# Hybrid mixer backbone on one core: latent branch reordered, gate tiles ahead of the transposes, raw gate tiles, norm sums in buffers of their own

## The reference, cut to what matters

```
def qkv(dq, dkv, kr, rope_tabs, need_q):
    kv = (rms_norm(dkv, g_ckv) @ w_ukv).reshape(b, t, MLA_HEADS, MLA_NOPE + MLA_V)
    k  = rms_norm(concatenate([kv[..., :MLA_NOPE], k_r], -1), g_k)
    q  = rms_norm((rms_norm(dq, g_cq) @ w_uq).reshape(b, t, MLA_HEADS, 96), g_q)
    ...
g = sigmoid(gate_pre)         # 3 x 1024 gate channels, from the same input as q, k, v
y = (g_a * y_a + g_b * y_b + g_c * y_c) @ w_out
```

## Time and profile before

| | us |
|---|---|
| median of 3 runs (1823.93 to 1825.36) | 1824.24 |
| the profiled execution's own time | 1828.72 |
| its span in the profile | 1827.0 |
| latent branch, layer 0, first product to first score (439.60 to 593.06) | 153.5 |
| latent branch, layer 1 (1414.71 to 1526.76) | 112.1 |
| PE busy, share of the span | 1659.8, 91% |
| DVE, ACT, POOL busy | 969.2, 783.1, 668.7 |
| granted PE clock, mean (1 is 2.4 GHz) | 0.961 |

### The profile page before, as it was taken

One profiled execution on the slowest core, in us unless ns is written; L12 is line 12 of the kernel. 1 busy time (PEld: TensorE's weight loads), 2 busy tenths in 40 slices (PEclk: granted clock), 3 DMA queues, 4 the chain that ended last, 5 costly groups with the idle time before them and its releaser, 6 DMA issues.

```text
span 1827.0 us, 24655 instructions
## 1 busy us (share of the span) xinstructions
PE 1659.8 (91%) x9536; PEld 1394.2 (76%) x9536; DVE 969.2 (53%) x1751; ACT 783.1 (43%) x1484; POOL 668.7 (37%) x389
## 2 busy tenths in 40 slices
PE   7998989899878999899999998978899788889998
PEld 3876779767666667688888886968887676789998
DVE  5855816753235555359496964143135145556665
ACT  4334644343446442442323234247534465455443
POOL 0633344411234001345455543525541343034443
PEclk9999999999989999999999998989999898999999
DMA  8432434400122312224354743223420133245553
GB/s 334 188 138 89 177 113 170 150 24 24 61 87 89 125 66 100 77 92 164 136 200 169 276 165 112 87 81 108 130 93 24 65 121 126 79 139 185 185 184 116
DMA packets 69852, 230.63 MB, mean 126 GB/s; under 512 B 18281, under 2 KB 24809, under 8 KB 56425
## 3 DMA queue, kind: packets, MB, share of 16 engines
q1 hardware_dynamic: 60880, 213.67, 33.4%
q10 hardware_dynamic: 8856, 15.39, 2.4%
HBM read 216.45 MB, written 12.58 MB: 125 GB/s over the span
## 4 chain that ended last, share of the span: by engine, by line
PE 72%; DVE 10%; ACT 9%; issue 4%; POOL 3%; DMA 1%; SPq 0%; ACTq 0%; POOLq 0%; DVEq 0%
PE bank L1694 36%; PE bank L1732 8%; PE bank L1776 7%; PE bank L1714 4%; PE bank L2044 4%; PE bank L2023 3%; PE bank L1758 2%; PE bank L2030 2%; ACT wH L772 2%; POOL wL L659 1%; DVE acc L1165 1%; PE bank L1925 1%; DVE mjunk L1162 1%; ACT L798 1%; POOL wL L661 1%
## 5 line engine op out<-in xcount | busy, mean ns | idle before, releaser
L659 POOL TENSOR_TENSOR wL<-raw,wH 128x1280 fp32r<-128x1280 f32 (+4 forms) x146 | 307.8, 2108 | 612.3 <-ACT wH L772 612.3
L772 ACT ACTIVATE wH<-raw 128x768 fp32r<-128x768 f32 (+7 forms) x396 | 296.7, 806 | 486.0 <-PE bank L1694 351.1
L661 POOL TENSOR_TENSOR wL<-raw,wH 128x768 fp32r<-128x768 f32 (+3 forms) x198 | 322.8, 1630 | 368.5 <-ACT wH L772 368.4
L1694 PE MATMUL bank<-hH,wH 128*128 128x512 f32 (+1 forms) x720 | 246.8, 343 | 4.6 <-DVE oL L1557 2.9
L1694 PE MATMUL bank<-hL,wH 128*128 128x512 f32 (+1 forms) x720 | 245.2, 341 | 0.0
L1694 PE MATMUL bank<-hH,wL 128*128 128x512 f32 (+1 forms) x720 | 245.1, 340 | 0.0
L1694 PE MATMUL bank<-oH,wH 128*128 128x512 f32 (+1 forms) x576 | 197.0, 342 | 2.9 <-DVE oL L1557 2.9
L1694 PE MATMUL bank<-oL,wH 128*128 128x512 f32 (+1 forms) x576 | 195.7, 340 | 0.0
L1694 PE MATMUL bank<-oH,wL 128*128 128x512 f32 (+1 forms) x576 | 195.6, 340 | 0.0
L1165 DVE SCALAR_TENSOR_TENSOR acc<-acc,cb 128x1024 f32<-128x1024 f32 x88 | 170.9, 1955 | 2.5
L1732 PE MATMUL bank<-hH,wH 128*128 128x512 f32 (+1 forms) x384 | 142.4, 371 | 25.7 <-ACT gst L798 12.3
(11 more groups left out here) (217 smaller groups left out, 3258.3 us busy)
## 6 DMA issues: line engine op xcount, KB each, us to landing
raw<-in_p_ff SPq DMA_DIRECT2D x64, 1024.0 KB, 4.8
acc<-in_p_mod SPq DMA_DIRECT2D x44, 1024.0 KB, 5.7
raw<-in_p_ml SPq DMA_DIRECT2D x12, 1024.0 KB, 5.3
raw<-in_p_na SPq DMA_DIRECT2D x12, 1024.0 KB, 5.6
raw<-in_p_mgc SPq DMA_DIRECT2D x16, 512.0 KB, 3.6
raw<-in_p_mga SPq DMA_DIRECT2D x16, 512.0 KB, 3.5
raw<-in_p_mgb SPq DMA_DIRECT2D x16, 512.0 KB, 3.5
raw<-in_p_out SPq DMA_DIRECT2D x8, 1024.0 KB, 4.8
```

The source lines that it names most:

```text
L659: pool.tensor_tensor(l_[:, 0:cut], r_[:, 0:cut], h_[:, 0:cut].bitcast(F32), ALU.subtract)
L661: pool.tensor_tensor(l_[:, cut:k * w], r_[:, cut:k * w], h_[:, cut:k * w].bitcast(F32), ALU.subtract)\
L772: act.activation(flat(wH, n)[:, part], flat(raw, n)[:, part], ACT.Copy)\
L1694: ins = pe.matmul(dst, w_[:, kk, c:c + P], r_[:, kk, lo:TOK], start=kk == k0 and m == 0, stop=kk == k0 + kn - 1 and m == 2)
```

## The change

It concerns the latent branch of both layers, the gate tiles in it, and the start of `to`. What it does, part by part:

- **Norm.** ACT squares the first four chunks straight from PSUM, each into a buffer of its own (c_sq), and PE's sums stand between and behind the two halves of dk; the sum of the fifth stands between the two `cn` gate tiles. Chunks 0 to 2 (queries) and 3, 4 (keys) get their roots, scaling and split separately, and PE's first unit waits for the first three alone. The rotary key's squares are one instruction at the start, its sums one instruction, and its rotation stands ahead of DVE's work on the fifth chunk. Ln and Exp come after one table load.
- **Gate tiles.** `cn` has 2 in both layers (3 and 4 before); the units have 1 each in layer 0 (0, 2, 0, 1, 1, 1, 1, 1 before) and 2, 2, 1, 1, 1, 1 in layer 1 (1 each before). In a unit they stand ahead of the transposes. Tiles 16 to 23 are copied out raw (Copy in place of Tanh).
- **Units.** ACT does both squares, both roots, then the weight splits, the gates, and the two query copies of the unit before; DVE both sums, the two key copies of the unit before, then both scalings.
- **Merge.** ACT makes 8 Tanh over chunks of the branch-1 gate at the start of `to`, 4 ahead, into g_tanh; DVE waits for them.
- **Ring.** The order of blocks follows the new order, and with it the planner's slots. By L444 to L458 the changed releasers are, for layer 0 / 1: gate 16 by dk (both); gate 17 by gate 14 (both); uq0 by dq1 (both); gate 18 (layer 1), gate 19 (layer 0) by uq0; ukv (layer 1) by uq1 instead of gate 18; gate 20 (layer 1) by gate 18; wo0 by to2 instead of to1 (both); wo1 (layer 1) by wo0 instead of to3, since in layer 1 it now overlaps wo0's slots.

The diff, cut to its core:

```diff
-FILL = (dict(chain=3, loop=8, last=3, cn=3, units=(0, 2, 0, 1, 1, 1, 1, 1)),
-        dict(chain=3, loop=8, last=3, cn=4, units=(1, 1, 1, 1, 1, 1)))
+FILL = (dict(chain=3, loop=8, last=3, cn=2, units=(1, 1, 1, 1, 1, 1, 1, 1)),
+        dict(chain=3, loop=8, last=3, cn=2, units=(2, 2, 1, 1, 1, 1)))
+
+
+def untouched(l, T):
+
+    return T >= gate_range(l, 0).start
...
-        at = gate_range(l, 0).start
-        if l == 0:
-            load += [("uq", l, 0), g[at], g[at + 1], ("uq", l, 1), ("ukv", l, 0), *g[at + 2:]]
-            use += [("uq", l, 0), g[at], g[at + 1], ("uq", l, 1), *g[at + 2:at + 6], ("ukv", l, 0), *g[at + 6:]]
-        else:
-            load += [("uq", l, 0), g[at], ("uq", l, 1), g[at + 1], ("ukv", l, 0), *g[at + 2:]]
-            use += [("uq", l, 0), g[at], ("uq", l, 1), *g[at + 1:at + 5], ("ukv", l, 0), *g[at + 5:]]
+        stages = [("uq", l, k // 2 if l == 0 else k) for k in range(4 if l == 0 else 2)] + [("ukv", l, 0)] * 4
+        for k, key in enumerate(stages):
+            fill = [g[T] for T in gate_range(l, k)]
+            load += ([key] if stages.index(key) == k else []) + fill
+            use += ([key] if key not in stages[k + 1:] else []) + fill
...
+        c_sq = (s_sq, s_sq2, st[:, 0], st[:, 1], view(10752, 512))
...
+                    if untouched(l, T):
+                        ins = act.activation(gst[:, n % 2, t0:], bk, ACT.Copy)
+                    else:
+                        ins = act.activation(gst[:, n % 2, t0:], bk, ACT.Tanh, scale=0.5)
+                    ins.then_inc(S("gate_free").handle, 1)
...
-                        for j in range(3):
-                            ahead(N[("dq", l, j) if j < 2 else ("dk", l, 0)])
-                            if j < 2:
-                                for b in range(2):
-                                    c = 2 * j + b
-                                    lo = t0 if c < 3 else 0
-                                    act.activation(l_c[:, c, lo:], full(u0 + j, b)[:, lo:TOK], ACT.Copy)\
-                                        .then_inc(free(u0 + j, b), 1)
-
-                        for u, b in ((u0 + 1, 1), (u0 + 2, 1)):
-                            act.wait_ge(*S(f"bank_free{2 * (u % 2) + b}").at(u // 2 + 1))
-                        for c in range(5):
-                            lo = t0 if c < 3 else 0
-                            if c > 0:
-                                act.wait_ge(*S(tag + "csum").at(c))
-                            act.activation(s_sq[:, lo:], l_c[:, c, lo:], ACT.Square).then_inc(S(tag + "csq").up(1), 1)
-                        act.wait_ge(*S(tag + "csum").at(5))
-                        act.activation(st[:, 0, t0:], bank[4][:, t0:TOK], ACT.Ln, scale=1.0 / MLA_QR, bias=eps[:, 0:1])
-                        link(act.activation(st[:, 1, :], bank[5][:, :], ACT.Ln, scale=1.0 / MLA_KVR, bias=eps[:, 0:1]))
-                        act.activation(st[:, 0, t0:], st[:, 0, t0:], ACT.Exp, scale=-0.5)\
-                            .then_inc(S(tag + "cstd").up(1), 1)
-                        act.activation(st[:, 1, :], st[:, 1, :], ACT.Exp, scale=-0.5)\
-                            .then_inc(S(tag + "cstd").up(1), 1)
-                        act.preload_act_table_set("sqrt_and_others")
-                        for c in range(5):
+                        act.activation(l_t, small[:, :, 32:64], ACT.Square).then_inc(S(tag + "krs").up(1), 1)
+                        exp_and_ln()
+                        for j in range(2):
+                            for b in range(2):
+                                c = 2 * j + b
+                                lo = t0 if c < 3 else 0
+                                src = full(u0 + j, b)[:, lo:TOK]
+                                act.activation(c_sq[c][:, lo:], src, ACT.Square).then_inc(S(tag + "csq").up(1), 1)
+                                act.activation(l_c[:, c, lo:], src, ACT.Copy).then_inc(free(u0 + j, b), 1)
+                            ahead(N["dq", l, j])
+
+                        def deviations(q, lo, done):
+
+                            act.wait_ge(*S(tag + "csum").at(done))
+                            link(act.activation(st[:, q, lo:], bank[4 + q][:, lo:TOK], ACT.Ln,
+                                                scale=1.0 / (MLA_KVR if q else MLA_QR), bias=eps[:, 0:1]))
+                            act.activation(st[:, q, lo:], st[:, q, lo:], ACT.Exp, scale=-0.5)\
+                                .then_inc(S(tag + "cstd").up(1), 1)
+
+                        def latent_high(c):
+
                             lo = t0 if c < 3 else 0
                             act.wait_ge(*S(tag + "cn").at(c + 1))
                             act.activation(oH[:, C_AT[c], lo:], l_c[:, c, lo:], ACT.Copy).then_inc(S(tag + "cH").up(1), 1)
 
-                        for t in range(NTILE):
-                            act.activation(l_t[:, 0:ROPE], small[:, t, 32:64], ACT.Square).then_inc(S(tag + "krs").up(1), 1)
-                            act.wait_ge(*S(tag + "krsum").at(t + 1))
+                        deviations(0, t0, 3)
+                        act.wait_ge(*S(f"bank_free{2 * ((u0 + 2) % 2) + 1}").at((u0 + 2) // 2 + 1))
+                        act.activation(c_sq[4], l_c[:, 4, :], ACT.Square).then_inc(S(tag + "csq").up(1), 1)
+                        for c in range(3):
+                            latent_high(c)
+                        ahead(N["dk", l, 0])
+                        deviations(1, 0, 5)
+                        for c in (3, 4):
+                            latent_high(c)
                         gates_out(l, "cn")
+                        act.preload_act_table_set("sqrt_and_others")
...
+                    else:
+                        for k in range(len(nb) // 2):
+                            for m in (2 * k, 2 * k + 1):
+                                squared(m)
+                            for m in (2 * k, 2 * k + 1):
+                                deviation(m)
+                            u = u0 + 3 + k
+                            for key in (("uq", l, 0), ("uq", l, 1), ("ukv", l, 0)):
+                                if used[N[key]] == (f"bank_full{2 * (u % 2) + 1}", u // 2 + 1):
+                                    ahead(N[key])
+                            gates_out(l, k)
+                            if k:
+                                queries_out(2 * k - 2)
+                                queries_out(2 * k - 1)
+                        act.preload_act_table_set("exp_and_others")
...
+                def merge_tanh(c):
+
+                    act.wait_ge(*S(f"gate_b{c}").at(16 * (l + 1)))
+                    act.activation(g_tanh[:, c, t0:], m_raw[:, c, t0:], ACT.Tanh, scale=0.5)\
+                        .then_inc(S(f"mg{l}_tanh").up(1), 1)
+
+                for c in range(4):
+                    merge_tanh(c)
                 for j in range(4):
+                    for c in (2 * j + 4, 2 * j + 5):
+                        if c < KC:
+                            merge_tanh(c)
...
+                        dve.wait_ge(*S(tag + "krs").at(1))
+                        dve.reduce_sum(stat[:, 32:32 + NTILE], l_t, axis=AX)
+                        link(dve.tensor_tensor(l_kr, small[:, :, 32:64], ropeg[:, l, 1:2, :].broadcast_to([P, NTILE, ROPE]), ALU.mult))
+                        for t in range(2, NTILE):
+                            rope(l_kr[:, t:t + 1, :], l_kr[:, t:t + 1, :], l_r, t - 2, 1)
...
+                        for q, cs in ((0, (0, 1, 2)), (1, (3, 4))):
+                            dve.wait_ge(*S(tag + "cstd").at(q + 1))
+                            if q:
+                                dve.wait_ge(*S(tag + "csum").at(5))
...
+                        for k in range(len(nb) // 2):
+                            sums(2 * k)
+                            sums(2 * k + 1)
+                            if k:
+                                keys_out(2 * k - 2)
+                                keys_out(2 * k - 1)
+                            normalised(2 * k)
+                            normalised(2 * k + 1)
+                        keys_out(len(nb) - 2)
...
-                        dve.wait_ge(*S(f"gate_b{c}").at(16 * (l + 1)))
-                        free(dve.scalar_tensor_tensor(tmp, m_tanh[:, c, t0:], 1.0, full(u0 + j, b)[:, t0:TOK], ALU.add, ALU.mult),
+                        dve.wait_ge(*S(f"mg{l}_tanh").at(c + 1))
+                        free(dve.scalar_tensor_tensor(tmp, g_tanh[:, c, t0:], 1.0, full(u0 + j, b)[:, t0:TOK], ALU.add, ALU.mult),
...
-                        features(N["dk", l, 0], u0 + 2, KC, [(0, 0, 4, 0), (0, 4, 4, 0)], hH, hL)
-                        for c in range(5):
+
+                        def latent_sum(c):
+
                             lo = t0 if c < 3 else 0
                             pe.wait_ge(*S(tag + "csq").at(c + 1))
-                            pe.matmul(bank[4 if c < 3 else 5][:, lo:TOK], ones, s_sq[:, lo:TOK],
```

(24 more changed lines are left out.)

100 lines of the change are left out of this document (44 added, 56 removed).

## The result

The changed kernel takes **1778.13 us** (median of 4 runs, 1777.42 to 1778.3) against 1824.8 (4 runs, 1823.93 to 1825.82) for the kernel before on the same chip: ratio 0.9743, interval 0.9726 to 0.976. Forecast were 1772.4 and a range of 1763 to 1789. The profiled execution took 1777.42 us, its span is 1775.7.

The account below looks back on a forecast made before the run. PE, busy 91% of the span, was taken as the bound, with idle time and low clock in the latent stretches. -30.0 - 27.3 + 5.5 = -51.8 from 1824.2 gave 1772.4 us, range 1763 to 1789.

Parts of the forecast that it names:

- Layer 0, -30.0: Layer 0's latent branch: sums without waits, dense units and 5.2 us bare at the end, 123.5 against 153.5 us.
- The reason given for it: Layer 0's units: a unit and gate tile, 8.6 us, between transposes cover DVE; ACT takes about 6 of 9.6 without table switches.
- Layer 1, -27.3: Layer 1's latent branch: 79.0 us summed, plus waits at uq1 and ukv and clock, 84.8 against 112.1 us.
- the 5.8 allowed: Layer 1's weight splits of uq1 and ukv: 4.3 us of waits and 1.5 for the clock after them; bounds 0 and 9.
- wo, +5.5: Layer 1's wo: wo1 in wo0's slots loads late, PE starts 4.0 us later, plus 1.5 for the clock; bounds 3 and 9.
- Merge, 0: Start of `to`: ACT's eight Tanh are hidden, costing zero; 8.0 us if the cover went.
- Sum: Whole kernel: -30.0 - 27.3 + 5.5 = -51.8 us, taken from 1824.2, the median 4.5 below the profiled 1828.7.
- 2: Rival: DVE's chain exceeds its cover, rotary operations stretched beside POOL, about 2 us in 12 cycles; +24, 1796, chance 0.12→0.08.
- 1: Rival: ACT's and POOL's weight splits become the bound at uq1 and ukv in both layers; +14, 1786, chance 0.12.
- 3: Rival: the ring's new placement repeats, 35 blocks of layer 1's wo and ff each losing 4.0 us; +140, 1908, chance 0.02.

Follow-up runs that it names:

- e2: Changed kernel with Tanh back in the units' gate tiles and none at the start of the merge: 1778.55 us.
- e1: Changed kernel with transposes put back ahead of the gate tiles in latent units, ACT's and DVE's pairs kept: 1778.3 us.
- e7: Changed kernel with ACT and DVE going bank by bank through the units instead of in pairs, gate tiles still ahead of transposes: 1794.48 us.
- e12: Changed kernel with ACT and DVE bank by bank as in e7, and transposes ahead of the gate tiles: 1804.18 us.
- e4: Changed kernel with layer 1's to1 moved to ring slots 8 to 11, so wo0 and wo1 lie as before the change: 1774.18 us.
- e13: As e6, but only ukv's split meant to stand ahead of the roots; the edit missed that, in effect e4 again: 1773.58 us.
- e11: As e6, with the transposes ahead of the gate tiles again as in e1: 1775.06 us.
- e6: e4 with ACT's weight splits placed between the squares and the roots of a unit: 1772.15 us.

## Why the prediction was right, and where not

**Layer 0, -30.0.** Measured -30.3 (153.5 to 123.2). Sums without waits, dense units and a bare end (5.6 us, forecast 5.2) were as forecast.

**The reason given for it** was only half right. The text put the cover down to the unit and gate tile between two pairs of transposes, and to ACT's cycle without table switches. e2 shows that the switches cost nothing. e1 shows that the order is worth 0 to 2 us once ACT and DVE go in pairs; e7 and e12 show that the pairs, which the prediction did not price at all, are worth 16 to 26 us. With the new order they keep a weight split from standing behind a copy (e7); with the old one they keep a root from standing behind the next unit's square, and DVE's scaling out of POOL's way (e12). The change's name and its working part are not the same, and that layer 0 came out right for another reason is in part luck.

**Layer 1, -27.3.** Measured -20.9: the term that was mis-sized, by 6.4. The waits up to uq1 were 0.6 + 2.2 (forecast 2.8), that ahead of ukv 2.0 (1.3 to 1.5), but each of the two units behind them ran at the low level of the clock, 1.2 GHz, for most of its length (products of 384 columns 0.32 us apart instead of 0.17 until 1427.2, those of 512 0.43 instead of 0.23 until 1441.0): 4.96 and 4.58 us where 3.15 and 2.75 were dense. Together 8.5 against the 5.8 allowed, +2.7. Of the 5.8, 1.5 stood for the clock, called half of 2.6, which is 1.3; measured are 3.6. The first 96 products took 16.85 where other runs of the same code took 14.34: +2.5, which goes with no edit. The end was 6.6 bare, not 5.2: +1.4. The three make 6.6, the whole miss. How the 8.5 is made up varies too: in e4, whose code in this branch is the same, uq1 took 3.39 behind the same 2.2, but ukv waited 3.65 and took 5.46, 9.4 in all.

**wo, +5.5.** Measured +4.4 at wo2 (27.4 us after the first product of `to` before, 31.8 after), 3.5 by the end of the execution (305.4 against 302.0), and 4.0 by e4. wo1 started 2.7 us later, not 4.0, and took 7.51 instead of 5.76. The chain forecast (wo0's low part, landing, ACT, DVE) is the one in the rows.

**Merge, 0.** The first multiplication of DVE waited only for PE, and e2, which takes the eight Tanh away again, gained nothing.

**Sum.** Between the profiled executions the forecast was -51.8 and the measurement -51.3 (1828.72 to 1777.42), but only by luck: layer 1's miss was made good by 1.5 ahead of layer 0 and 2.1 between the branches, which nobody forecast, and by a loss at wo that was 2.0 smaller. Between the medians (1824.24 and 1778.13) it is -46.1: the profiled execution before lay 4.5 above its median, that after 0.7 below. Taking the whole 4.5 off the forecast moved it to 1772.4, 5.7 under the result.

**Rivals.** 2 was right in mechanism and small in effect here: in layer 1 DVE was stretched beside POOL, above all in two scalings, by some 6 us each (from 1421.16 and from 1435.77). The second cost PE nothing. The first made the roots late: of ukv's wait of 2.0 some 1.0 is from it (the sums start at 1430.37, the second square ends at 1429.43). In e4 they start at 1428.83, with the square ended at 1426.27, and the wait is 3.65. In e12 the same mechanism makes most of the long waits. The Trainium skill (SBUF — State Buffer, SBUF: two separate sides) has a DVE operation with two SBUF inputs and a GpSimd operation that reads SBUF lock each other out for a whole instruction; the trace agrees, 5.24 against 0.49. Of 1 only layer 1's half came, and 3 did not repeat: waits for a low part only at wo0 (1.5) and wo1 (2.98).

## What to carry to other kernels

Look in each engine's own list for an instruction that waits for the *next* unit and stands ahead of one that finishes *this* unit: here a root behind the next square, and a weight split behind a copy that waits for the next unit. They cost 16 to 26 us, where 19 us of table loads off the path cost none. An engine that comes late can also run into another's work: here DVE's scaling came beside POOL's subtractions. Order within a list and order between engines are priced together, since one is free only while the other is in time. And after any change of filler or loading order, read which block now lands in whose slots: one planner decision gave 4 us away in `wo`, far from the part that was reordered.

## What the runs showed of the hardware

**The same products take 817.6 to 823.9 us** between the two branches, in fourteen executions. e13 and e11, whose programs are the same there, in the view of stretches:

```profile
560.39:1384.15 823.76, 773.00 (x4101) 641.47 (x4101) 440.56 (x715) 322.23 (x596) 326.38 (x163) 0.97 0.35 122
```

```profile
562.05:1379.61 817.56, 766.85 (x4100) 635.47 (x4101) 440.61 (x715) 323.42 (x597) 328.30 (x167) 0.97 0.35 123
```

DVE and ACT are busy as long, PE 6.2 us longer: it is time of PE's products, and in one stretch of 40 us the granted clock was 0.93 in e13 and 1.00 in e11. It goes with no edit. A gain smaller than this spread, as e6's, can't be read from the total of one profile.

**DVE beside POOL** takes 0.29 or up to 2.48 us for one and the same operation (128x128), 0.49 or 5.24 for four of 128x32; POOL's own times hardly change in the two branches (1.81 to 1.87 for uq's part of 128x768). The stretch is not a slower rate but a wait for the end of POOL's instruction. In the changed kernel, DVE and then POOL:

```profile
1435.77 1.83 DVE L1529 TENSOR_TENSOR arena<-arena,ropeg 128x128 f32<-128x128 f32 x1
1437.63 1.53 DVE L1265 TENSOR_TENSOR arena<-arena,const 128x128 f32<-128x128 f32 x1
...
1435.10 2.35 POOL L665 TENSOR_TENSOR wL<-raw,wH 128x1024 fp32r<-128x1024 f32 x1
1437.41 1.60 POOL L663 TENSOR_TENSOR wL<-raw,wH 128x640 fp32r<-128x640 f32 x1
```

The DVE operations end at 1437.60 and 1439.16, POOL's at 1437.45 and 1439.01: 0.15 us apart both times. All 13 operations of this size with both inputs in SBUF that began during a subtraction of POOL in the two branches ended 0.15 us behind it. DVE's scaling, whose first input is in PSUM (L1524, `bank`), began during one 12 times in the execution and was never stretched: 0.56 us at 1435.18, beside POOL, as at 1428.32, without it. So what a rotary step costs beside POOL is what is left of POOL's instruction at that moment, and POOL's for uq and ukv are 1.0 to 2.5 us long. It goes the other way too, where DVE begins first: at wo0 DVE's large part of the low copy (1542.16 + 1.49) is under way when POOL starts its own 128x768 at 1543.01, and that takes 2.35 us instead of 1.8, as in the earlier trace rows.
